# First attention's scores in one stretch of four heads over four PSUM banks

## The reference

```python
kb = band(k)      # previous block of 128 keys and the block itself
vb = band(v)
s = jnp.einsum('bnqkgd,bnckd->bnkgqc', qb, kb) * (HEAD_DIM ** -0.5)
s = jnp.where(valid, s, -jnp.inf)
m = jnp.maximum(jnp.max(s, axis=-1, keepdims=True), sink)
e = jnp.exp(s - m)
probs = e / (jnp.sum(e, axis=-1, keepdims=True) + jnp.exp(sink - m))
o = jnp.einsum('bnkgqc,bnckd->bnqkgd', probs, vb)
```

## Time and profile before

| | |
|---|---|
| median of 3 runs | 952.77 us (952.4 to 953.79) |
| profiled execution | 952.9 us, span 950.9 us |
| TensorE busy | 937.4 us, 99% |
| VectorE busy | 534.8 us, 56% |
| ScalarE busy | 470.4 us, 49% |
| HBM read | 221.54 MB, 234 GB/s over the span |
| mean granted TensorE clock | 0.997 |

### The profile page before, as it was taken

One profiled execution on the slowest core, in us unless ns is written; L12 is line 12 of the kernel. 1 busy time (PEld: TensorE's weight loads), 2 busy tenths in 40 slices (PEclk: granted clock), 3 DMA queues, 4 the chain that ended last, 5 costly groups with the idle time before them and its releaser, 6 DMA issues.

```text
span 950.9 us, 14068 instructions
## 1 busy us (share of the span) xinstructions
PE 937.4 (99%) x5793; PEld 762.6 (80%) x5793; DVE 534.8 (56%) x842; ACT 470.4 (49%) x727; POOL 4.2 (0%) x13
## 2 busy tenths in 40 slices
PE   9999999999999999999999999999999999999996
PEld 8989787888889999999889888889876665666553
DVE  5888896775766555555586875676454212122213
ACT  5588665757345444544567756445452131313113
POOL 1000000000000000000000000000000000000000
PEclk9999999999999999999999999999999999999998
DMA  9945465435555555554645635466757999999993
GB/s 321 310 139 174 152 236 191 139 128 173 172 174 207 184 177 177 177 180 149 213 149 175 233 131 167 143 248 238 269 188 300 409 409 408 409 409 408 409 410 116
DMA packets 89862, 223.55 MB, mean 235 GB/s; under 512 B 9162, under 2 KB 14019, under 8 KB 89795
## 3 DMA queue, kind: packets, MB, share of 16 engines
q1 hardware_dynamic: 87488, 219.62, 63.9%
q10 hardware_dynamic: 2306, 2.99, 0.9%
HBM read 221.54 MB, written 1.05 MB: 234 GB/s over the span
## 4 chain that ended last, share of the span: by engine, by line
PE 85%; DVE 6%; ACT 3%; issue 2%; DMA 2%; SPq 1%; ACTq 0%; DVEq 0%
PE pb L493 18%; PE pb L495 18%; PE pb L494 18%; PE pb L2492 12%; PE pb L2515 6%; PE pb L2532 3%; PE pb L2466 2%; DMA raw<-in_w_in 2%; DVE wl L1561 2%; PE pb L583 2%; ACT wh L1016 1%; PE pb L663 1%; PE pb L651 1%; PE pb L727 1%; PE pb L634 1%
## 5 line engine op out<-in xcount | busy, mean ns | idle before, releaser
L1561 DVE TENSOR_TENSOR wl<-raw,wh 128x2048 fp32r<-128x2048 f32 (+3 forms) x112 | 246.3, 2207 | 97.6 <-ACT wh L1016 97.3
L1016 ACT ACTIVATE wh<-raw 128x2048 fp32r<-128x2048 f32 (+3 forms) x112 | 206.5, 1852 | 108.0 <-PE pb L495 99.1
L493 PE MATMUL pb<-wh,th 128*128 128x512 f32 (+2 forms) x620 | 246.4, 397 | 0.5 <-DVE wl L1561 0.3
L495 PE MATMUL pb<-wh,tl 128*128 128x512 f32 (+2 forms) x620 | 238.9, 385 | 0.0
L494 PE MATMUL pb<-wl,th 128*128 128x512 f32 (+2 forms) x620 | 238.6, 385 | 0.0
L493 PE MATMUL pb<-th,wh 128*128 128x256 f32 x528 | 152.7, 289 | 0.0
L494 PE MATMUL pb<-tl,wh 128*128 128x256 f32 x528 | 149.3, 283 | 0.0
L495 PE MATMUL pb<-th,wl 128*128 128x256 f32 x528 | 149.3, 283 | 0.0
L493 PEld LDWEIGHTS pb<-wh,th 128*128 128x128 f32 x620 | 116.5, 188 | 25.2 <-DVE wl L1561 2.5
L495 PEld LDWEIGHTS pb<-wh,tl 128*128 128x128 f32 x620 | 116.4, 188 | 23.5
L494 PEld LDWEIGHTS pb<-wl,th 128*128 128x128 f32 x620 | 116.7, 188 | 20.5
(11 more groups left out here) (418 smaller groups left out, 1123.9 us busy)
## 6 DMA issues: line engine op xcount, KB each, us to landing
raw<-in_w_in SPq DMA_DIRECT2D x31, 1024.0 KB, 5.2
raw<-in_w_up SPq DMA_DIRECT2D x16, 1024.0 KB, 5.6
raw<-in_w_down SPq DMA_DIRECT2D x16, 1024.0 KB, 5.1
raw<-in_w_exp_gate SPq DMA_DIRECT2D x9, 1024.0 KB, 18.7
raw<-in_w_xkv SPq DMA_DIRECT2D x8, 1024.0 KB, 5.1
raw<-in_w_exp_down SPq DMA_DIRECT2D x8, 1024.0 KB, 17.5
raw<-in_w_exp_up SPq DMA_DIRECT2D x7, 1024.0 KB, 15.2
my<-in_w_exp_down SPq DMA_DIRECT2D x7, 1024.0 KB, 16.7
```

The source lines that it names most:

```text
L493: PE.matmul(o, lh, rh, start=start, stop=False, skip_group_check=True)
L495: return PE.matmul(o, ll, rh, start=False, stop=stop, skip_group_check=True)
L1016: ACTE.activation(hi_of(i), raw_of(i), ACT.Copy).then_inc(S["hi"], 1)
L1561: DVE.tensor_tensor(lo_of(i), raw_of(i), hi_of(i).bitcast(F), ALU.subtract).then_inc(S["lo"], 1)
```

## The change

The scores of the first attention's four heads are made in one stretch: first t = 1 of all four heads, into banks 0 and 1, then t = 0 of all four, into banks 2 and 3, two heads side by side in each bank. For n of 2 and 3 the stretch waits for `o_lo` at 2(n-1) and `pt` at 4(n-1), for n = 1 for the memory's turns. VectorE adds the mask bank by bank, two heads at once. Places move, and so do the orders of ScalarE and VectorE. The transposes of probabilities use banks 0 and 1 in place of 2 and 0. The old forms stay for n of 4 and 5, as `pe_scores2` and `dve_masked2`.

```diff
-        def pe_scores(n, two):
+        def pe_scores(n):
+            if n == 0:
+                PE.wait_ge(S["kq_T"], 6)
+            else:
+                PE.wait_ge(S["sc_add"], 4 * n)
+            if n == 1:
+                PE.wait_ge(S["turn_lo"], TB_["mem"] + 8)
+            if n >= 2:
+                PE.wait_ge(S["pt"], 4 * (n - 1))
+                PE.wait_ge(S["o_lo"], 2 * (n - 1))
+            for t in (1, 0):
+                w = 128 * (t + 1)
+                for i, h in enumerate(heads_of(n)):
+                    c = w * (i // 2)
+                    m = PE.matmul(PB[i % 2 + 2 * (1 - t)][:, c:c + w], att_lhs(n, h, t), att_rhs(n, h, 0, w), start=True, stop=True,
+                                  skip_group_check=True)
+                    if i >= 2:
+                        m.then_inc(S["sc_mm"], 1)
...
@@ pe_turn_probs, act_probs
-                b = (2, 0)[i % 2]
+                b = i % 2
...
@@ places
-                pe_turn("mem", v3(RB, 2, D), chunks, banks=(2, 3), free=lambda b: [(S["kq_T"], 6)])
+                pe_turn("mem", v3(RB, 2, D), chunks, banks=(2, 3), free=lambda b: [(S["sc_add"], 4)])
...
-                       (0, 1): {1: scores_0, 5: lambda: pe_scores(0, 1)},
+                       (0, 1): {2: lambda: pe_scores(0)},
...
-            at_xkv = {(0, 0): {0: lambda: pe_scores(1, 0), 4: lambda: pe_scores(1, 1)},
-                      (0, 1): {1: values_0, 5: lambda: pe_turn_probs(0, 1)},
-                      (1, 0): {1: lambda: pe_values(0), 2: lambda: pe_scores(2, 0), 5: lambda: pe_scores(2, 1)},
-                      (1, 1): {1: lambda: pe_turn_probs(1, 0, 12), 5: lambda: pe_turn_probs(1, 1)},
-                      (2, 0): {0: lambda: pe_values(1), 2: lambda: pe_scores(3, 0), 5: lambda: pe_scores(3, 1)},
-                      (2, 1): {1: lambda: pe_turn_probs(2, 0, 16), 5: lambda: pe_turn_probs(2, 1)},
-                      (3, 0): {0: lambda: pe_values(2)},
+            at_xkv = {(0, 0): {4: lambda: pe_scores(1)},
+                      (0, 1): {3: values_0, 6: lambda: pe_turn_probs(0, 1)},
+                      (1, 0): {1: lambda: pe_values(0), 5: lambda: pe_scores(2)},
+                      (1, 1): {3: lambda: pe_turn_probs(1, 0, 12), 6: lambda: pe_turn_probs(1, 1)},
+                      (2, 0): {1: lambda: pe_values(1), 5: lambda: pe_scores(3)},
+                      (2, 1): {3: lambda: pe_turn_probs(2, 0, 16), 6: lambda: pe_turn_probs(2, 1)},
+                      (3, 0): {1: lambda: pe_values(2)},
                       (3, 1): {2: lambda: pe_turn_probs(3, 0), 6: lambda: pe_turn_probs(3, 1)}}
...
@@ act_main
             act_unit("w_xkv_2", 0, 1)
+            act_probs(0, 1)
             act_exps(1, 0)
-            act_probs(0, 1)
...
                 act_unit("w_xkv_2", n, 1)
+                act_probs(n, 1)
                 if n < 3:
                     act_exps(n + 1, 0)
-                act_probs(n, 1)
...
+        def dve_masked(n):
+            SS = SSV[n].rearrange("p (h n) -> p h n", h=4)
+            if n in (2, 3):
+                DVE.wait_ge(S["pt_mm"], 4 * (n - 2) + 4)
+            for b, (i, w, o) in enumerate(((0, 256, 128), (1, 256, 128), (0, 128, 0), (1, 128, 0))):
+                DVE.wait_ge(S["sc_mm"], 4 * n + b + 1)
+                DVE.tensor_tensor(SS[:, i::2, o:o + w], v3(PB[b], 2, w), cst("mask1", w, o).unsqueeze(1).to_broadcast([128, 2, w]),
+                                  ALU.add).then_inc(S["sc_add"], 1)
...
@@ dve_main
             dve_unit("w_rnn_proj", 0, 0)
-            dve_masked(0, 0)
+            dve_masked(0)
             dve_unit("w_rnn_proj", 0, 1)
-            dve_masked(0, 1)
             dve_max(0)
...
-            dve_masked(1, 0)
             dve_unit("w_rnn_proj", 1, 1)
-            dve_masked(1, 1)
+            dve_masked(1)
...
             for n in (1, 2, 3):
-                if n < 3:
-                    dve_masked(n + 1, 0)
                 dve_probs(n)
                 dve_values(n - 1)
                 if n < 3:
-                    dve_masked(n + 1, 1)
+                    dve_masked(n + 1)
                     dve_max(n + 1)
```

More of the change, by code:

```diff
@@ L621, in pe_turn_q, with pe_scores2 @@
             m.then_inc(S["kq_mm"], 1)
-        def pe_scores(n, two):
+        def pe_scores(n):
[16 more added lines that the diff above has]
+                        m.then_inc(S["sc_mm"], 1)
+        def pe_scores2(n, two):
             for i in (2 * two, 2 * two + 1):
@@ L628, in pe_scores @@
                     PE.wait_ge(S["sc_add"], 4 * n + i - 1)
-                elif n not in (0, 4):
-                    if i == 0 and n not in (1, 5):
-                        PE.wait_ge(S["pt"], 4 * (n - 2) + 4)
+                elif n == 5:
                     PE.wait_ge(S["sc_add"], 4 * (n - 1) + 3 + i)
@@ L806, in turn_mem @@
                     PE.wait_ge(S["mem_scaled"], 2)
-                pe_turn("mem", v3(RB, 2, D), chunks, banks=(2, 3), free=lambda b: [(S["kq_T"], 6)])
-            def scores_0():
-                PE.wait_ge(S["kq_T"], 6)
-                pe_scores(0, 0)
+                pe_turn("mem", v3(RB, 2, D), chunks, banks=(2, 3), free=lambda b: [(S["sc_add"], 4)])
             def values_0():
@@ L919, in scores_4 @@
                 PE.wait_ge(S["t2"], 8)
-                pe_scores(4, 0)
+                pe_scores2(4, 0)
             at_gates = {(0, 0): {6: lambda: pe_turn2(0, lambda t, h: QM[:, t, 96 * h:96 * h + 96])},
@@ L924, in pe_main @@
                         (1, 0): {4: scores_4},
-                        (1, 1): {0: lambda: pe_scores(4, 1), 3: pe_pool, 5: lambda: pe_scores(5, 0)},
-                        (2, 0): {1: lambda: pe_scores(5, 1)},
+                        (1, 1): {0: lambda: pe_scores2(4, 1), 3: pe_pool, 5: lambda: pe_scores2(5, 0)},
+                        (2, 0): {1: lambda: pe_scores2(5, 1)},
                         (2, 1): {4: lambda: (PE.wait_ge(S["pool_lo"], 4), pe_turn_probs(4, 0, 24)),
@@ L1141, in act_probs @@
                     ACTE.wait_ge(S["val_mm"], 4 * n)
-                ACTE.activation(AREA[n][i], PB[(2, 0)[i % 2]][:, 0:384], ACT.Copy).then_inc(S["pt"], 1)
+                ACTE.activation(AREA[n][i], PB[i % 2][:, 0:384], ACT.Copy).then_inc(S["pt"], 1)
         def act_values(n, free=None):
@@ L1720, in dve_rope, with dve_masked2 @@
                         DVE.tensor_tensor(o, tmp[2 * j], tmp[2 * j + 1], (ALU.subtract, ALU.add)[j]).then_inc(S["rope"], 1)
-        def dve_masked(n, two):
+        def dve_masked(n):
             SS = SSV[n].rearrange("p (h n) -> p h n", h=4)
-            if n in (2, 3) and two == 0:
+            if n in (2, 3):
                 DVE.wait_ge(S["pt_mm"], 4 * (n - 2) + 4)
+            for b, (i, w, o) in enumerate(((0, 256, 128), (1, 256, 128), (0, 128, 0), (1, 128, 0))):
+                DVE.wait_ge(S["sc_mm"], 4 * n + b + 1)
+                DVE.tensor_tensor(SS[:, i::2, o:o + w], v3(PB[b], 2, w), cst("mask1", w, o).unsqueeze(1).to_broadcast([128, 2, w]),
+                                  ALU.add).then_inc(S["sc_add"], 1)
+        def dve_masked2(n, two):
+            SS = SSV[n].rearrange("p (h n) -> p h n", h=4)
             if n == 4 and two == 0:
@@ L1730, in dve_masked @@
                 DVE.wait_ge(S["sc_mm"], 4 * n + i + 1)
-                DVE.tensor_tensor(SS[:, i], PB[i % 2][:, 0:384], cst("mask1" if n < 4 else "mask2", 384),
-                                  ALU.add).then_inc(S["sc_add"], 1)
+                DVE.tensor_tensor(SS[:, i], PB[i % 2][:, 0:384], cst("mask2", 384), ALU.add).then_inc(S["sc_add"], 1)
         def dve_max(n):
@@ L2313, in dve_main @@
             DVE.wait_ge(S["t2"], 8)
-            dve_masked(4, 0)
-            dve_masked(4, 1)
+            dve_masked2(4, 0)
+            dve_masked2(4, 1)
             dve_unit("gates2", 1, 1)
@@ L2321, in dve_main @@
                                          chunk(TH[1], g).bitcast(F), ALU.mult, ALU.subtract).then_inc(S["pool_lo"], 1)
-            dve_masked(5, 0)
-            dve_masked(5, 1)
+            dve_masked2(5, 0)
+            dve_masked2(5, 1)
             dve_max(5)
```

## The result

The changed kernel takes **963.35 us** (median of 5 runs, 962.68 to 965.82) against 953.55 for the kernel before beside it (952.4 to 953.86): a ratio of 1.0114, 95% interval 1.0103 to 1.0126. It is slower by some 10 us. The forecast was 959.9 with a range of 958.9 to 963.9: the sign and the mechanism came out, the size did not: +7.1 us forecast, +9.8 in the medians. Rival B (963.9), not case A, is what happened.

What follows compares the result with a forecast made beforehand. TensorE's own queue was taken as the bound. Gain -1.6, stalls +4.15, +4.26 and +0.35 sum to +7.1 us on the profiled 952.9, giving 960.0, less 0.1 to the median: 959.9 us, range 958.9 to 963.9.

Steps and rivals of the forecast that it cites:

- Rival B: Clock falls to half rate in both long stalls, 2.0 us lost after each: 963.9 us; chance 0.34.
- case A: The sum as computed, with no clock loss: 959.9 us, own range 959.0 to 961.0; chance 0.50.
- The stretch: Four heads' scores in one overlapping stretch: 1.72 us against 2.12, gaining 0.40 for each of four blocks, 1.6 us.
- Case D: The four heads' scores don't overlap: 1.3 us a block more, 5.2 in all, 965.1 us; chance 0.05.
- The wait for `o_lo`: TensorE's scores of blocks 2 and 3 wait for VectorE's subtraction of values: stalls of 4.15 and 4.26 us.
- everything ScalarE does after hangs behind a later place: ScalarE copies the second half before the next block's first exponentials, so its later work follows a later TensorE place; unpriced separately.
- Case C: The wait for `o_lo` is already met, leaving only the 1.6 us gain: 951.2 us; chance 0.06.
- Block 3's turn: Turn of block 3's probabilities, kept at place 2 of (3, 1), waits for `dve_probs(3)`: stall 0.35 us.
- The other waits met: Remaining new waits, of scores of blocks 0 and 1, memory's turns and `pe_values(0)`, are met when TensorE arrives: no cost.
- The masks at nothing: VectorE's mask adds by bank, 2.0 us before and after, moved later: no cost; some 2 us a block without cover.
- The tail moves as a whole: A shift at 190 to 230 us reaches the kernel's end, as no long transfer runs ahead on its own.

Runs made afterwards that it cites:

- e5: e1, plus VectorE's masks of block n+1 before block n's probabilities (n = 1, 2) and block 3's first turn moved from place 2 to 3: 951.55 us, ratio 0.998.
- e3: Kernel before, plus a wait for `o_lo` ahead of the second pair of scores of n = 2 and 3: 958.72 us, ratio 1.0058.
- e1: Changed kernel, but for n = 1, 2 ScalarE takes the values right after evicting `w_xkv_2`, VectorE subtracts them before `dve_probs`: 952.62 us, ratio 0.9999.
- e4: Changed kernel with ScalarE's old order, the next block's first exponentials before the copies of the second two heads' transposes: 963.37 us, ratio 1.0111.
- e6: Changed kernel with the wait for `o_lo` moved inside the stretch, between t = 1 and t = 0: 961.64 us, ratio 1.0087.
- e2: Changed kernel with 31 (n = 2) and 35 (n = 3) additional unread matmuls before the wait for `o_lo`: 960.29 us, ratio 1.0078.
- e7: e3 with 15 additional unread matmuls in front of each wait for `o_lo`: 956.99 us, ratio 1.0038.

## Why the prediction was off, point by point

**The stretch: right.** Forecast 1.72 us and overlap of the four heads, measured 1.70; forecast gain 1.6, measured 1.66 in the trace and 1.7 in the medians of e5. Case D is rejected.

**The wait for `o_lo`: right.** 4.15 and 4.26 forecast, 3.80 and 4.26 measured. The subtraction ended at 195.06 in place of 195.53, since this execution ran 0.4 us ahead before the change had begun. TensorE should have come 0.4 sooner as well, but had lost 0.3 of it at the start of unit (1, 0), so its last record before the stall ends at 191.41, about where I had forecast its arrival. That makes the stall shorter than forecast; the 0.3 was paid a little earlier. e3 shows that the wait alone is enough, e1 that without it the stalls go, e4 that ScalarE's swapped order isn't the cause. My sentence that "everything ScalarE does after hangs behind a later place" is true, but it is a matter of a few tenths. Case C is rejected.

**Block 3's turn: right,** 0.35 forecast, 0.40 measured. **The other waits met: not quite.** The 0.3 us at unit (1, 0) stands in no term of my sum. I had checked TensorE's earlier arrival against the scores, turns and values, but not against the banks of the main stream.

**The choice of A over B: wrong, and this is the step that failed.** My sum put the half-rate work behind the stalls at nothing; it measured 3.7 us. I held against B that "it needs nearly the whole of each stall". That came from one fall, after 4.0 us of idleness at the kernel's end, which I read as the time that a fall takes. The runs show falls 2.0 us and 3.7 us after TensorE's last record ended (193.4 and 217.3), and one at 195.84 after an idle time of 1.89. All eight unfilled stalls of 1.89 us and more, in four profiled executions (the changed kernel, e3, e4, e6), brought a fall, in the stall or within 1.6 us after it; by the mean clocks of e3's other executions, probably not every stall of 1.9 us does. A single fall seen at the end of a trace says how long idleness once lasted, not how little is enough. Had B been the likeliest, as it should have been, its 963.9 would have been 0.6 from the median. Its price came out near, 4.0 us forecast, 3.7 measured in the profiled execution and 3.1 in the medians (e2), but that is partly luck: it rested on an assumption that no row showed, two equal losses of 2.0, and they were 2.3 and 1.4. The Trainium skill ("TensorE: Matmul & The Clock Gate", Part 1) says that after idling it takes sustained work to get the full rate back; the trace agrees, with the clock at 0.50 for 5.0 us of work after the first stall and 2.9 us after the second. I named this rule and gave it too little weight. (My range began at 958.9, while A's own low end was 959.0; nothing hangs on it.)

**The masks at nothing: right only by the stall's cover.** In the changed kernel they held up no stretch and no turn, as forecast. In e1, where the stall is gone, they cost 0.7 us. In all versions they may also have part in the 0.3 us at unit (1, 0): block 1's adds, half of which VectorE did in idle time before, now come after the split of weights, ahead of line 1806. No run takes this apart. I had priced the case without cover at "some 2 us a block", and put no condition on when it would come.

**The tail moves as a whole: right.** The attention's stretch grew by 10.8 us and the span by 10.5, with the 0.4 us named above between them.

## What to carry to other kernels

Where an insertion is moved to other PSUM banks, ask who reads these banks last and what stands ahead of that reader in its own queue: here a finished result sat in a bank for over 6 us because its reader was queued behind an unrelated step. Draining the bank before the long steps took the time back to that of the kernel before (+1.1% to no difference, e1), and two more moves brought it to -0.2% (e5). Then look for the next wait that the long one had hidden. Price a stall of TensorE twice, as a wait and as half-rate work behind it; by the runs here 1.9 us of idleness already brought the second in some executions, and 1.13 us did not.

## What the runs showed of the hardware that was not expected

* TensorE's granted clock fell after an idle time of only 1.89 us, and 0.4 us after the work had begun again (e3), in e6 1.6 us after it. A stall can be over before its second price begins.
* Matmuls whose result nobody reads made the kernel faster: 66 of them by 3.1 us (e2), 30 by 1.7 us (e7).
* Two row groups of 64 partitions run side by side over four heads as over two: 16 records in 1.58 us, with the way in and out, 0.40 us, paid once.
